# The rounding copy of the gated rows moved from VectorE to ScalarE, with other work of VectorE between the product and its low part

## What is computed

```python
def hierarchical_moe(u, w_router_group, w_router_expert, w_gate, w_up, w_down):
    ...
    combine = (g_onehot[:, :, None] * (p_g[:, :, None] * w_in_group[:, None, :])).astype(x.dtype)
    y = jnp.zeros_like(x)
    for g in range(N_GROUPS):
        hid = jax.nn.silu(jnp.einsum('nd,edf->nef', x, w_gate[g])) * jnp.einsum('nd,edf->nef', x, w_up[g])
        y = y + jnp.einsum('nef,efd->nd', hid * combine[:, g, :, None], w_down[g])
    return y.reshape(B_, S_, D)
```

## Time and profile before

| | us |
|---|---|
| median of 3 runs | 2482.16 |
| lowest and highest run | 2480.53, 2486.57 |
| the profiled execution's own time | 2479.27 |
| its span | 2477.5 |
| TensorE busy in the span | 2328.5 (94%) |
| VectorE busy | 1872.3 (76%) |
| ScalarE busy | 1355.1 (55%) |

### The profile page before, as it was taken

The page is one execution under the profiler, slowest core; times in us unless marked ns, Lnnn a source line. Parts: engine busy times, 40 slices in busy tenths (PEclk is TensorE's granted clock), DMA queues, the critical chain, the costliest instruction groups (busy, mean ns, idle before and its releaser), DMA issues.

```text
span 2477.5 us, 29734 instructions
## 1 busy us (share of the span) xinstructions
PE 2328.5 (94%) x11078; PEld 1722.1 (70%) x11078; DVE 1872.3 (76%) x2183; ACT 1355.1 (55%) x1497; POOL 20.5 (1%) x39
## 2 busy tenths in 40 slices
PE   7998999999997978999999998999989999988998
PEld 6566877777775455777877776556587965834987
DVE  2745999999997464999999998877467755574665
ACT  3234988898885143988888885136433312102332
POOL 0000000000000000000000001000000000000000
PEclk9998999999998998999999999999999999998999
DMA  9313989988896311999888998553155842632460
GB/s 329 120 68 133 378 361 373 385 361 361 361 373 254 136 69 68 373 373 375 361 362 362 373 383 307 173 186 132 61 215 207 308 141 86 220 119 77 174 234 18
DMA packets 115417, 603.67 MB, mean 244 GB/s; under 512 B 5208, under 2 KB 8352, under 8 KB 90556
## 3 DMA queue, kind: packets, MB, share of 16 engines
q1 hardware_dynamic: 111536, 588.83, 61.3%
q0 software_dynamic: 3792, 13.62, 1.6%
HBM read 601.38 MB, written 1.05 MB: 243 GB/s over the span
## 4 chain that ended last, share of the span: by engine, by line
PE 54%; DVE 20%; issue 13%; ACT 9%; DMA 2%; DVEq 1%; SPq 0%; ACTq 0%
PE bank L950 11%; DVE slab_parts L2639 9%; ACT high L1865 6%; PE bank L1260 4%; PE bank L1582 3%; PE bank L1212 3%; PE bank L1076 3%; PE bank L1239 3%; PE bank L1201 2%; PE bank L1511 2%; PE bank L1513 2%; PE bank L1512 2%; PE bank L1492 2%; PE bank L1494 2%; PE bank L1493 2%
## 5 line engine op out<-in xcount | busy, mean ns | idle before, releaser
L2639 DVE TENSOR_TENSOR slab_parts<-ring,high 128x2048 fp32r<-128x2048 f32 x384 | 862.0, 2286 | 33.0 <-ACT high L1865 31.0
L1865 ACT ACTIVATE high<-ring 128x2048 fp32r<-128x2048 f32 x384 | 728.1, 1916 | 41.4 <-PE bank L1212 34.1
L1709 ACT ACTIVATE arena<-bank 128x512 f32<-128x512 f32 (+4 forms) x174 | 95.5, 588 | 399.4 <-PE bank L1582 91.2
L1212 PE MATMUL bank<-high,xT_parts 128*128 128x512 f32 x1024 | 292.8, 408 | 18.0 <-DVE slab_parts L2639 14.1
L1212 PE MATMUL bank<-slab_parts,xT_parts 128*128 128x512 f32 x1024 | 278.2, 393 | 0.0
L950 PE MATMUL bank<-ring,xT 128*128 128x512 f32 (+3 forms) x576 | 239.0, 576 | 8.9 <-ACT xT L1709 4.0
L1212 PEld LDWEIGHTS bank<-high,xT_parts 128*128 128x128 f32 x1024 | 183.6, 189 | 78.4 <-DVE slab_parts L2639 38.5
L1212 PEld LDWEIGHTS bank<-slab_parts,xT_parts 128*128 128x128 f32 x1024 | 193.0, 188 | 45.2
L1871 ACT ACTIVATE arena<-bank 64x512 f32<-64x512 f32 (+2 forms) x352 | 185.0, 534 | 57.0 <-PE bank L1239 51.6
L950 PEld LDWEIGHTS bank<-ring,xT 128*128 128x128 f32 x576 | 111.0, 194 | 134.7 <-issue 124.1
L2307 DVE TENSOR_TENSOR slab_parts<-ring,high 128x2048 fp32r<-128x2048 f32 x64 | 145.7, 2289 | 60.4 <-ACT high L1729 59.8
(11 more groups left out here) (373 smaller groups left out, 3494.8 us busy)
## 6 DMA issues: line engine op xcount, KB each, us to landing
ring<-in_moe_w_gate SPq DMA_DIRECT2D x64, 2048.0 KB, 8.4
ring<-in_moe_w_up SPq DMA_DIRECT2D x64, 2048.0 KB, 9.4
ring<-in_moe_w_down SPq DMA_DIRECT2D x64, 2048.0 KB, 9.2
ring<-in_mlp_w SPq DMA_DIRECT2D x32, 2048.0 KB, 12.8
ring<-in_w_mod SPq DMA_DIRECT2D x24, 2048.0 KB, 9.0
ring<-in_even_w_in SPq DMA_DIRECT2D x7, 2048.0 KB, 21.2
ring<-in_odd_w_in SPq DMA_DIRECT2D x6, 2048.0 KB, 10.6
ring<-in_h_w_in SPq DMA_DIRECT2D x6, 2048.0 KB, 8.3
```

The lines of the kernel that those rows point to most:

```text
L1212: last = mm(dst[:, :], seated2[:, 4 * half + k, e], part_[:, k, :], start=(half == a == k == 0), stop=(half == a == 1 and k == 3))
L1865: act_fn(hi, weight_half(layer, name, half), ACT.Copy).then_inc(sem(f"high{layer}"), 1)
L2639: v.tensor_tensor(low, w, hi.bitcast(F32), ALU.subtract).then_inc(sem(f"low{layer}"), 1)
```

## The change

`hide` is taken apart. The product stays where it was on VectorE. The cast becomes `hide_high`, a copy on ScalarE that waits until the product has left its bank. The remainder becomes `hide_low` on VectorE, which waits for ScalarE by the semaphore `hidden_high`. For expert 0, `hide_low` stands behind `weigh`; `hide_high` stands behind the turned weights and ahead of gate1. For expert 1 both stand in the next round: `hide_low` behind the first low part for gate0's follower, `hide_high` behind the first high part, ahead of the copy out of gate0. After round 15 both stand ahead of the last down product.

```diff
+        h4 = pair_h.rearrange("p (f c) -> p f c", f=4)
...
+                def hide_high(e, r):
+                    moe_empty(act, layer, filling(f"fold{e}", r))
+                    act_fn(hidden2[:, :, 0], h4, ACT.Copy).then_inc(sem(f"hidden_high{layer}"), 1)
+
                 def into(name, w, r, first, last):
                     refill(name, r, 0, first, last)
+                    if name == "gate0" and not first:
+                        hide_high(1, r - 1)
                     out_of(name, r, raw[:, w, :].rearrange("p (f q) -> p f q", f=4),
                            lambda ps: ps[:, :].rearrange("p (q f) -> p f q", f=4))
                     refill(name, r, 1, first, last)
...
                     silu(0, r)
                     if not first:
                         turn_weights(r)
+                    hide_high(0, r)
                     into("gate1", 0, r, first, last)
...
                 round_(PAIRS - 1, last=True)
+                hide_high(1, PAIRS - 1)
                 down(1, 0, PAIRS, more=False)
...
-                    steps = sem(f"hide_step{layer}")
...
-                    moe_empty(dve, layer, u)
-                    v.tensor_copy(hidden2[:, :, 0], h4_).then_inc(steps, 1)
-                    dve.wait_ge(steps, r * 2 + (e + 1))
-                    v.tensor_tensor(hidden2[:, :, 1], h4_, hidden2[:, :, 0].bitcast(F32), ALU.subtract)\
+
+                def hide_low(e, r):
+
+                    dve.wait_ge(sem(f"hidden_high{layer}"), r * 2 + (e + 1))
+                    v.tensor_tensor(hidden2[:, :, 1], h4, hidden2[:, :, 0].bitcast(F32), ALU.subtract)\
                         .then_inc(sem(f"hidden{layer}"), 1)
...
                 def round_(r, first=False, last=False):
-                    refill("gate0", r, first, last)
+                    make_low_after("gate0", r, 0, first, last)
+                    if not first:
+                        hide_low(1, r - 1)
+                    make_low_after("gate0", r, 1, first, last)
                     make_low_after("up0", r, 0, first, last)
...
                     weigh(r)
+                    hide_low(0, r)
                     refill("gate1", r, first, last)
...
                 round_(PAIRS - 1, last=True)
+                hide_low(1, PAIRS - 1)
                 add_rows(1, 0, PAIRS)
```

More of the change, by code:

```diff
@@ L2653, in hide @@
                     dve.wait_ge(sem(f"silu{layer}"), r * 2 + (e + 1))
-                    steps = sem(f"hide_step{layer}")
-                    h4_, s4 = (x.rearrange("p (f c) -> p f c", f=4) for x in (pair_h, pair_silu))
-                    v.tensor_tensor(h4_, s4, ps[:, 4 * SEATS:8 * SEATS].rearrange("p (f c) -> p f c", f=4), ALU.mult)\
+                    s4 = pair_silu.rearrange("p (f c) -> p f c", f=4)
+                    v.tensor_tensor(h4, s4, ps[:, 4 * SEATS:8 * SEATS].rearrange("p (f c) -> p f c", f=4), ALU.mult)\
                         .then_inc(moe_drained[layer][u.bank], 1)
-                    moe_empty(dve, layer, u)
-                    v.tensor_copy(hidden2[:, :, 0], h4_).then_inc(steps, 1)
-                    dve.wait_ge(steps, r * 2 + (e + 1))
-                    v.tensor_tensor(hidden2[:, :, 1], h4_, hidden2[:, :, 0].bitcast(F32), ALU.subtract)\
+                def hide_low(e, r):
+                    dve.wait_ge(sem(f"hidden_high{layer}"), r * 2 + (e + 1))
+                    v.tensor_tensor(hidden2[:, :, 1], h4, hidden2[:, :, 0].bitcast(F32), ALU.subtract)\
                         .then_inc(sem(f"hidden{layer}"), 1)
```

## The result

The changed kernel takes 2509.95 us in the median of five runs (2509.31 to 2514.08), the kernel before 2482.16 of five (2480.53 to 2486.57). The ratio is 1.0117 with an interval of 1.0101 to 1.0132: 1.2% slower. The forecast was 2503 and slower. The profiled execution of after took 2509.95 with a span of 2508.2, so the two profiles lie 30.7 us apart, 2.9 more than the medians.

A forecast was written before the change was run, and what follows sets the result against it. A closed path bounds the round: M to L by TensorE, then ScalarE; L to next M by VectorE. Adding 0.70 less 0.06 a round, plus end rounds, gave 20.8 us for both layers: 2503 us, range 2491 to 2514.

The forecast's parts named there:

- main term: ScalarE's new copy for expert 0 waits for VectorE's product and delays the queue behind it: 0.70 us a round longer.
- M: Start of a round's first product on VectorE, 520.13 in the round followed before the change.
- L: Start of VectorE's gapless stretch to the next product, after its 0.66 us wait for ScalarE's high copy; M + 15.61 before.
- 3.37 us of idle time: ScalarE's waits of 1.75, 0.30 and 1.32 us for TensorE's gathers and first down product, forecast to absorb most of the shift.
- rival "faster": ScalarE's idle time covers the wait if the high copy starts before M - 0.10; round 33.90, 2471.6 us; chance 0.05.
- the queue's length from round 0: ScalarE's queue from the high copy to L with nothing to wait for, read in layer 0's round 0: 15.58 us.
- The path over TensorE: TensorE's fold of expert 1 shifts by about 0.5 us and gate0 to about M + 15.08, with no new loss.
- Expert 1's copy: Behind L, ScalarE's queue shifts by 0.30 us, leaving 0.06 of the 0.33 us spared by VectorE's cast.
- No overlap at the new copies: Rival: ScalarE's new copies have no start under the preceding copy's end; 0.90 us a round, 2511 us; chance 0.20.
- no change: Rival: ScalarE's queue to L some 0.4 us shorter than in round 0; within 0.3%, some 2487 us; chance 0.12.
- I give them 0.70 each: First and last round of each layer have the same wait ahead of the same queue: 0.70 us each.
- Nothing outside the experts changes: Stretches outside the two layers' expert rounds add no time to the forecast: 0 us.

The follow-up runs named there:

- e1_expert0: The changed kernel with expert 1's cast back on VectorE, so only expert 0's copy is on ScalarE: 2510.35 us, 34.88 a round.
- e4_copy_no_wait: The kernel before plus an unused 128x256 copy, waiting for nothing, at the place of expert 0's new copy on ScalarE: 2479.53 us, 34.22 a round.
- e7_behind_one: The changed kernel with expert 0's copy one place later on ScalarE, behind gate1's first high part and ahead of the copy out of gate1: 2478.66 us.
- e2_expert1: The changed kernel with expert 0's cast back on VectorE, so only expert 1's copy is on ScalarE: 2481.85 us, 34.22 a round.
- e9_delay29: The kernel before with 29 unused additions on VectorE ahead of layer 0's experts: 2504.35 us, 205.3 us between the layers.
- e10_delay10: The kernel before with 10 unused additions on VectorE ahead of layer 0's experts: 2487.15 us, 198.9 us between the layers.

## Why the prediction was right, and where it was short

**The main term was right.** The copy starts at M + 0.44, as worked out, and the high part behind it at M + 0.77 (forecast M + 0.73): the copy takes 0.418 and not 0.40. From the high part to L it is 15.49 (forecast 15.58, from the earlier trace rows). M to L: 16.26, forecast 16.31. e1_expert0 and e4_copy_no_wait show that the copy of expert 0 costs it, and only with its wait, and e7_behind_one that it is the place of the wait: there the shift of what follows is smaller than the 3.37 us of idle time, which was the criterion of the rival "faster".

The prediction took the queue's length from round 0 and not from the idle time, and that was the better way. The shift is 4.24 us (from M - 3.47 to M + 0.77); less 3.37 of idle time that leaves 0.87, and 0.65 were measured. The rest is in starts under the end of the instruction before. At the gathers the kernel before had waits in place of them; in the changed kernel gather 0 starts 0.11 ahead of the high part's end and gather 1 0.12 ahead of gather 0's, and down0's lower rows 0.02 behind.

**The path over TensorE was right.** fold1 was to start some 0.5 later, at M + 13.28, and gate0 at M + 15.08. Timeline of TensorE, after:

```profile
295.12 2.00 PE L1230 MATMUL bank<-arena 128*128 128x64 f32 x16 [0.31 <-ACT xT_parts L1872]
296.92 1.18 PE L1213 MATMUL bank<-high,xT_parts 128*128 128x512 f32 x4
```

That is M + 13.25 and M + 15.05, and ScalarE's high part behind it comes at M + 17.28 (forecast 17.31). The wait at the fold is 0.31 us; about 0.5 was forecast.

**Expert 1's copy was right in kind.** ScalarE's copy out of gate0 is at L + 3.32 (forecast 3.28) and `add_rows` at L + 10.45 (forecast 10.39), and L to M is 18.61, where it was 18.62: 0.01 of the spared cast is left, not 0.06. e2_expert1 shows it alone. This miss and the one of 0.05 at M to L have opposite signs, so that their difference, 0.64 us for this round, came out as forecast.

**The rivals.** No overlap at the new copies: fell. At both places the next instruction starts 0.09 and 0.10 ahead of the copy's end (282.73 and 282.64; 301.55 and 301.45). The Trainium skill, "ScalarE: Activation LUTs", section "What ACT_TABLE_LOAD costs", gives about 93 ns for this, and the trace agrees here. The 0.40 us estimated from that section's figures for the copy are 0.02 under the 0.418 measured. Faster and no change fell with M to L at 16.26: the first needed the high part before M - 0.10, the second a queue some 0.4 us shorter than 15.58, and it is 0.09 shorter.

**The first rounds were short by 1.2 us.** The step that failed is "I give them 0.70 each". In round 0 the idle time of 3.37 isn't there, and its high part ran 0.37 ahead of its M (246.52 in the earlier trace rows, the product of that round at 246.89). It now runs at M + 0.77, so 1.14 later, and no idle time covers any of it: M to L grows from 15.21 (262.10) to 16.26 (263.19). Another 0.13 is behind L, where VectorE now waits for ScalarE. Timeline of ScalarE in round 0, after:

```profile
247.37 0.42 ACT L1890 ACTIVATE hidden_parts<-arena 128x256 fp32r<-128x256 f32 x1 [1.32 <-DVE arena L2664]
247.70 1.90 ACT L1866 ACTIVATE high<-ring 128x2048 fp32r<-128x2048 f32 x1
```

Measured are 1.18 and 1.38 us more in the two layers; the 0.20 between them is the kernel before's, whose round 0 takes 33.76 and 33.56, while e4_copy_no_wait, e9_delay29 and e10_delay10 have 33.76 to 33.78 in both. The shift for the loop had been taken against a queue that has slack, and the same value was given to the one round that has none.

**The last rounds were short by 2.1 us.** "0.70 each" again. The product of expert 1 comes 0.79 later behind round 15's M (783.24 − 770.21 = 13.03 against 12.24), and its remainder 0.11 more, since nothing lies between product and remainder there: VectorE waits for the copy. These 0.90 us are in both layers. The larger part of layer 0's 2.45 is what follows. Timeline of TensorE at the end of layer 0, after:

```profile
784.62 1.52 PE L1240 MATMUL bank<-high,hidden_parts 128*128 128x512 f32 x4 [3.16 <-DVE hidden_parts L2670]
785.94 1.91 PE L1240 MATMUL bank<-slab_parts,hidden_parts 128*128 128x512 f32 x4
```

The table of stretches for the last down products, after (columns as in the earlier trace rows):

```profile
784.60:790.20 5.60, 5.58 (x18) 4.35 (x18) 0.69 (x1) 0.60 (x2) 0.00 (x0) 0.70 0.64 235
```

The same work before, in the timeline of TensorE:

```profile
773.07 1.20 PE L1239 MATMUL bank<-high,hidden_parts 128*128 128x512 f32 x4 [2.34 <-DVE hidden_parts L2661]
```

and in the table of stretches:

```profile
773.05:777.10 4.05, 4.04 (x18) 3.21 (x18) 0.68 (x1) 0.59 (x2) 0.00 (x0) 1.00 1.05 387
```

TensorE had stood still for 3.16 us instead of 2.34, and the same 18 matmuls ran at a granted clock of 0.70 instead of 1.00, 1.55 us longer. That the longer stand brought the lower clock isn't shown. In layer 1 the kernel before has nearly the short stand and the slow matmuls:

```profile
1526.35 2.07 PE L1239 MATMUL bank<-high,hidden_parts 128*128 128x512 f32 x4 [2.37 <-DVE hidden_parts L2661]
```

So it had 24.83 us for this end already, and the changed kernel takes 25.89 there: only 1.06 more. In the traces of all kernels here, the eight ends with a stand of 3.04 to 3.16 us all ran at the lower clock (0.58 to 0.70 in the mean), but so did seven of the twenty with 1.91 to 2.49 us (0.70 to 0.72). How much of the 1.55 us is the change's, and how much the one execution of the kernel before, stays open.

**"Nothing outside the experts changes" was wrong in time, though right in instructions.** The 4.8 us between the layers go with the granted clock, as shown above. The 0.9 behind them has no cause shown; over all kernels here that part takes 936.5 to 941.2 us with the same instructions. The remaining 0.9 is in the loop: its mean round was 34.21 before, where the sum used 34.23 (0.6 us over 28 rounds), and is 34.88 after, where the sum had 34.87 (0.3 us).

Altogether 1.2 + 2.1 + 4.8 + 0.9 + 0.9 = 9.9 us, which is what the profiled run has over the forecast made on the profiled run before (2509.95 against 2500.1). Against the forecast of the median, 2503, it is 7.0. That this stays in the range is in part luck: the upper end, 2514, had been set for a missing overlap and for a copy of 0.60 us, and neither came; the room was taken up by the ends of the layers and by the stretches outside the experts, for which the sum had nothing or too little.

## What to carry to other kernels

An instruction that is moved to another in-order engine costs there what its wait and it together hold up: 0.42 us of copying were free where nothing had to be waited for, and the same copy behind a stand until M + 0.44 cost 0.65 us a round. Compare the start that the wait and the instruction allow with the start that the next instruction had, and set the difference against the slack of the queue behind it, best by the same queue in a round where it waits for nothing; let the work that is already ready pass first. Find out in which part of a round the freed engine sets the length before its work is counted as a gain, and cost the first and the last round of a loop by their own rows, since the slack of the loop isn't there.

## What the runs showed of the hardware

Within one kernel's small edits, a stretch of identical instructions (578 matmuls) took 198.9 to 205.3 us, by a mean granted clock of 0.85 to 0.90. The difference of two profiles can so hold some 5 us in a stretch where no instruction differs; here that was a sixth of it. The 18 matmuls of the last down products took 4.05 us at full clock and 5.60 at 0.70.

A copy of 128x256 on ScalarE takes 0.418 us out of SBUF (64 of them, 0.416 to 0.422) and 0.38 out of PSUM (the group of the copies out of banks in the changed kernel):

```profile
L1872 ACT ACTIVATE arena<-bank 128x256 f32<-128x256 f32 x96 | 33.4, 380 | 3.1 <-PE bank L1230 2.3
```

The start under the end of the copy before isn't there at every pair of ScalarE's instructions. In the kernel before, all 90 high parts that follow a copy of 64x512 without a wait start 0.02 us after its end, and the 156 that follow a copy of 128x512 start 0.10 to 0.13 ahead of it. What decides this is open.
